# Expert products on four 32-column tiles of TensorE, from weights as loaded

## What is computed

```python
def moe_swiglu(x, w_router, w_gate, w_up, w_down):
    logits = (x @ w_router).astype(jnp.float32)
    top_vals, top_idx = lax.top_k(logits, TOP_K)
    weights = jax.nn.softmax(top_vals, axis=-1)
    combine = jnp.sum(jax.nn.one_hot(top_idx, N_EXPERTS) * weights[..., None], axis=-2)
    out = jnp.zeros_like(x)
    for e in range(N_EXPERTS):
        out = out + combine[..., e:e + 1] * swiglu(x, w_gate[e], w_up[e], w_down[e])
    return out
```

## Time and profile before

| | us |
|---|---|
| median of three runs | 1660.54 (1660.43 to 1660.86) |
| the profiled execution | 1658.83 |
| its span, first to last instruction | 1657.0 |
| TensorE busy in the span | 1598.1 |
| VectorE busy | 1284.6 |
| ScalarE busy | 1027.1 |
| moved by DMA | 464.09 MB |

### The profile page before, as it was taken

One profiled execution on the slowest core, in us unless ns is written; L12 is line 12 of the kernel. 1 busy time (PEld: TensorE's weight loads), 2 busy tenths in 40 slices (PEclk: granted clock), 3 DMA queues, 4 the chain that ended last, 5 costly groups with the idle time before them and its releaser, 6 DMA issues.

```text
span 1657.0 us, 20954 instructions
## 1 busy us (share of the span) xinstructions
PE 1598.1 (96%) x7543; PEld 1327.3 (80%) x7543; DVE 1284.6 (78%) x1060; ACT 1027.1 (62%) x837; POOL 41.3 (2%) x47
## 2 busy tenths in 40 slices
PE   7999999998999979999999999999999999999986
PEld 6887788887788868888888888888888888888865
DVE  5776555557745579889889889889889889889887
ACT  4433543444445457777777777777777777777762
POOL 3011000001000010000000000000000000000011
PEclk9999999999999979999999999999999999999998
DMA  9864555463453219999999999999999999989970
GB/s 368 294 263 132 183 198 182 166 214 127 161 201 102 77 51 361 368 336 356 371 337 361 376 327 352 381 330 351 379 334 352 379 333 366 379 316 368 365 280 26
DMA packets 194867, 464.09 MB, mean 280 GB/s; under 512 B 7456, under 2 KB 7472, under 8 KB 194320
## 3 DMA queue, kind: packets, MB, share of 16 engines
q1 hardware_dynamic: 192448, 453.01, 75.1%
q0 software_dynamic: 2384, 10.60, 1.6%
HBM read 462.53 MB, written 1.05 MB: 280 GB/s over the span
## 4 chain that ended last, share of the span: by engine, by line
PE 87%; DVE 7%; issue 3%; ACT 2%; DMA 1%; ACTq 0%; DVEq 0%
PE ps L1372 83%; DVE wl L858 2%; PE ps L1820 1%; PE ps L1389 1%; DVE acc L896 1%; DVE acc L1301 1%; ACT wh L538 1%; DVE htl L868 0%; DMA ws_raw<-in_gm_w_s_dram 0%; DVE stats L905 0%; PE ps L1700 0%; DVE ysl L1291 0%; ACT L538 0%; PE ps L1721 0%; PE ps L1592 0%
## 5 line engine op out<-in xcount | busy, mean ns | idle before, releaser
L858 DVE TENSOR_TENSOR wl<-raw,wh 128x2048 fp32r<-128x2048 f32 x372 | 844.8, 2288 | 132.1 <-ACT wh L538 131.7
L538 ACT CAST wh<-raw 128x2048 fp32r<-128x2048 f32 x372 | 712.6, 1917 | 263.2 <-PE ps L1372 263.1
L1372 PE MATMUL ps<-wh,xeh 128*128 128x512 f32 x896 | 355.0, 396 | 1.9 <-DVE wl L858 1.9
L1372 PE MATMUL ps<-wh,xel 128*128 128x512 f32 x896 | 350.0, 391 | 0.0
L1372 PE MATMUL ps<-wl,xeh 128*128 128x512 f32 x896 | 349.5, 390 | 0.0
L1372 PE MATMUL ps<-wh,hth 128*128 128x512 f32 x608 | 243.2, 400 | 8.7 <-DVE htl L868 4.4
L1372 PE MATMUL ps<-wl,hth 128*128 128x512 f32 x608 | 239.9, 395 | 0.0
L1372 PE MATMUL ps<-wh,htl 128*128 128x512 f32 x608 | 239.5, 394 | 0.0
L1372 PE MATMUL ps<-wh,bth 128*128 128x512 f32 x560 | 218.7, 391 | 1.8 <-DVE btl L868 1.6
L1372 PE MATMUL ps<-wh,btl 128*128 128x512 f32 x560 | 218.0, 389 | 0.0
L1372 PE MATMUL ps<-wl,bth 128*128 128x512 f32 x560 | 217.9, 389 | 0.0
(11 more groups left out here) (233 smaller groups left out, 1100.1 us busy)
## 6 DMA issues: line engine op xcount, KB each, us to landing
raw<-in_moe_w_gate_dram SPq DMA_DIRECT2D x114, 1024.0 KB, 6.9
raw<-in_moe_w_up_dram SPq DMA_DIRECT2D x112, 1024.0 KB, 7.0
raw<-in_moe_w_down_dram SPq DMA_DIRECT2D x112, 1024.0 KB, 6.3
raw<-in_gm_w_in_dram SPq DMA_DIRECT2D x14, 1024.0 KB, 14.6
raw<-in_ffn_w_gate_dram SPq DMA_DIRECT2D x14, 1024.0 KB, 5.0
raw<-in_ffn_w_up_dram SPq DMA_DIRECT2D x14, 1024.0 KB, 5.9
raw<-in_ffn_w_down_dram SPq DMA_DIRECT2D x14, 1024.0 KB, 4.8
raw<-in_fox_w_in_dram SPq DMA_DIRECT2D x12, 1024.0 KB, 5.1
```

What stands on the lines that cost most here:

```text
L538: nc.scalar.copy(wh[:, gs % SPL], raw[:, gs % RAW]).then_inc(s0["hi"], 1)
L858: nc.vector.tensor_tensor(wl[:, gs % SPL], raw[:, gs % RAW], wh[:, gs % SPL].bitcast(F32), ALU.subtract).then_inc(s0["lo"], 1)
L1372: return nc.tensor.matmul(o, a, b, start=start, stop=stop)
```

## The change

An expert now works on 96 slots (`CAP`), three groups of 32. The weights are not split: TensorE multiplies fp32 by fp32. One matmul has 32 slots as the stationary operand and 256 columns of weights as the moving one, and its output lies in one of four 32-partition strips of a PSUM bank, which places it on one of four 32-column tiles of TensorE. In gate and up (`gate_up`) the 256 columns are 128 of gate and 128 of up. Twelve matmuls cover 96 slots by 1024 columns for one row chunk of 128: strips 0 to 2 hold the three slot groups, strip 3 takes a fourth quarter of the columns for one group after the other; `t`, the strip, is the innermost loop. A block has 96 such matmuls for gate and up and 48 for down.

The 6 slots of `raw` and the room of `wh` and `wl` and two more slots become one ring of 14 slots of 1 MiB for the experts' loop, each with a semaphore of its own; SyncE reloads a slot once its granule has been used 14 granules before. The first 12 loads can go as soon as the slots are free, the last two after the gather.

The tokens of all experts are gathered once, before the loop: VectorE makes `every` (0/1, 256 tokens by 8 experts by 96 slots), TensorE does 64 matmuls of 384 columns, ScalarE and VectorE copy the 16 outputs out in turns to `xt`, and `expert_x` copies the next expert's part to `xe`. The outputs of an expert are unfolded from the four strips (`unfold`: five copies on ScalarE, three subtractions on VectorE) and their weighting moves behind the scatter (`add_weighted`). Hidden values: two SiLU and two multiplications per block, three transposes, one copy to `m_bt`; no `btl`. The loop over blocks is unrolled in the program. The branch for more tokens is taken if an expert has over 96.

Behind the loop ScalarE rounds the three first embedding granules before it unfolds the last expert's output, not after.

The core of the diff; what is left out are buffers, names, and the branch for more tokens:

```diff
+RING = 14
+CAP = 96
+G3 = 32
+    RING_SLOT = (4, 5, 0, 1, 2, 3, 8, 9, 10, 11, 6, 7, 12, 13)
+    GX_BANK = (0, 1, 4, 5, 6, 7, 0, 1, 4, 5, 6, 7, 4, 5, 6, 7)
...
+    def gu_at(j):
+        return G_BLK * j - 2 if j else 0
+    def down_at(j):
+        return G_BLK * j + 8 if j < NJ - 1 else G_EXP - 2
...
+        for idx in range(G_EXP):
+            if idx < RAW:
+                sp.wait_ge(streams[0]["lo"], G_MOE - RAW + 1 + idx)
+            elif idx < RING - 2:
+                sp.wait_ge(streams[0]["used"], G_MOE - (1 if idx < RING - 4 else 0))
+            elif idx < RING:
+                sp.wait_ge(gx_full, 2 * KD)
+            else:
+                sp.wait_ge(streams[0]["used"], G_MOE + idx - RING + 1)
+            ring_load(idx, ring_source(idx, 0))
+        def ring_loads(first, last, base):
+            with sp.Fori(first, last) as e:
                 g0 = sp.snap(G_MOE + e * G_EXP)
-                ex = sp.snap(e - rnd * NE)
-                swiglu_loads(G_MOE, g0, of(moe_w_gate, ex), of(moe_w_up, ex), of(moe_w_down, ex), True)
-                expert_head(g0 + G_EXP, sp.snap((ex + 1) % NE))
-        expert_head(G_MOE, 0)
-        experts(0)
+                ex = sp.snap(e - base)
+                for idx in range(G_EXP):
+                    source = ring_source(idx, ex)
+                    sp.wait_ge(streams[0]["used"], g0 + (idx - RING + 1))
+                    ring_load(idx, source)
...
+        def gathered(done):
             for half in range(2):
-                nc.scalar.mul(ysh[:, half * W:(half + 1) * W], ps[2 + half][:, :], wslot[:, 0:1])\
-                    .then_inc(done, 1)
-        def gathered(n):
-            for q in range(2):
-                act.wait_ge(gx_full, n * 2 - (1 - q))
-                nc.scalar.copy(xeh[:, 4 * q:4 * q + 4, :],
-                               ps[4 + q][:, :].rearrange("p (c t) -> p c t", t=P)).then_inc(gx_hi, 1)
-        def experts(rnd_no):
-            if rnd_no:
-                gathered(1 + rnd_no * (NE + 1))
-            with act.Fori(rnd_no * NE, (rnd_no + 1) * NE) as e:
+                for k in range(0, KD, 2):
+                    n = half * KD + k
+                    act.wait_ge(gx_full, done * (2 * KD) + (n + 1))
+                    nc.scalar.copy(xt[:, k, half * NQ:(half + 1) * NQ], ps[GX_BANK[n]][:, 0:NQ]).then_inc(gx_act, 1)
+        def unfold(ready, hi, fold, done):
+            act.wait_ge(s0["used"], ready)
+            nc.scalar.copy(ysh[0:CAP, 0:W], ps[2][0:CAP, :]).then_inc(hi, 1)
+            nc.scalar.copy(ysh[0:CAP, W:W + 2 * P], ps[3][0:CAP, 0:2 * P])
+            for q in range(3):
+                nc.scalar.copy(y_fold[q * G3:(q + 1) * G3, :], ps[2 + q // 2][CAP:P, q % 2 * 2 * P:(q % 2 + 1) * 2 * P])\
+                    .then_inc(fold, 1)
+            act.wait_ge(fold, done)
+            nc.scalar.copy(ysh[0:CAP, W + 2 * P:D], y_fold[0:CAP, :]).then_inc(hi, 1)
...
+                unfold(g0, y_hi, y_folded, e1 * 3)
+                for j in range(NJ):
+                    n = act.snap(e * NJ + (j + 1))
+                    act.wait_ge(s0["used"], g0 + (gu_at(j) + 4))
+                    nc.scalar.activation(m_sg[:, 0:2 * P].rearrange("p (q n) -> p q n", n=P),
+                                         ps[0][:, :].rearrange("p (q x) -> p q x", x=2 * P)[:, :, 0:P],
+                                         ACT.Silu).then_inc(e_silu, 1)
+                    nc.scalar.activation(m_sg[:, 2 * P:NQ], ps[1][:, 0:P], ACT.Silu).then_inc(e_silu, 1)
+                    act.wait_ge(h_turned, n)
+                    nc.scalar.copy(m_bt[:, j % 2, :, :], ps[4][:, 0:NQ].rearrange("p (c t) -> p c t", t=P))\
+                        .then_inc(bt_ready, 1)
+                    if j == 1:
+                        act.wait_ge(st_full, e1)
+                        nc.scalar.copy(sel_t[0:CAP, :], ps[6][0:CAP, 0:S]).then_inc(st_copied, 1)
...
+        for n in range(SPL):
+            round_hi(n, 1)
+        unfold(USED_TAIL + G_EXP, last_hi, last_folded, 3)
...
+        def gather(done, at_e):
             for half in range(2):
-                for c in range(4):
-                    last = mm(ps[2 + half][:, c * P:(c + 1) * P], zeros[:, :], zeros[:, :], c == 0, c == 3)
-            return last
-            pe.wait_ge(sel_ready, n * (T + 1) - 1)
-            for q in range(2):
-                for c in range(4):
-                    k = slice((4 * q + c) * P, (4 * q + c + 1) * P)
-                    o = ps[4 + q][:, c * P:(c + 1) * P]
+                pe.wait_ge(every_ready, at_e + half)
+                for k in range(KD):
+                    n = half * KD + k
+                    before = [b for b in range(n) if GX_BANK[b] == GX_BANK[n]]
+                    if before:
+                        b = before[-1]
+                        pe.wait_ge((gx_act, gx_dve)[b % 2], done * KD + (b // 2 + 1))
+                    o = ps[GX_BANK[n]][:, 0:NQ]
                     for m in range(T):
-                        mm(o, xh[:, m, k], sel[:, m, :], m == 0, False)
-                        last = mm(o, xl[:, m, k], sel[:, m, :], False, m == T - 1)
-                last.then_inc(gx_full, 1)
+                        one = every[:, m, 4 * half:4 * half + 4, :].rearrange("p e s -> p (e s)")
+                        mm(o, xh[:, m, k * P:(k + 1) * P], one, m == 0, False)
+                        last = mm(o, xl[:, m, k * P:(k + 1) * P], one, False, m == T - 1)
+                    last.then_inc(gx_full, 1)
...
+                def gate_up(j):
                     for half in range(2):
+                        idx = gu_at(j) + 2 * half
+                        slot = landed(idx)
+                        assert landed(idx + 1) == slot + 1
                         for c in range(4):
                             k = 4 * half + c
+                            for q in range(3):
+                                for t in range(4):
+                                    grp, n0 = (t, q) if t < 3 else (q, 3)
+                                    o = ps[q // 2][t * G3:(t + 1) * G3, q % 2 * 2 * P:(q % 2 + 1) * 2 * P]
+                                    last = mm(o.rearrange("p (x n) -> p x n", x=2), xe[:, k, grp * G3:(grp + 1) * G3],
+                                              ring[:, slot:slot + 2, c, n0 * P:(n0 + 1) * P], k == 0 and q != 1,
+                                              k == KD - 1 and q != 0)
+                        last.then_inc(s0["used"], 2)
+                def hidden_turn(j):
+                    pe.wait_ge(e_hid, pe.snap(e * NJ + (j + 1)))
+                    for c in range(3):
+                        last = nc.tensor.transpose(ps[4][:, c * P:(c + 1) * P], m_hb[:, c * P:(c + 1) * P],
                                                    ident[:, :])
+                    last.then_inc(h_turned, 1)
...
+                def down(j, k):
+                    if k == 0:
+                        pe.wait_ge(bt_ready, pe.snap(e * NJ + (j + 1)))
+                    slot = landed(down_at(j) + k)
+                    for kk in range(2):
+                        c = 2 * k + kk
+                        for q in range(3):
+                            for t in range(4):
+                                grp, n0 = (t, q) if t < 3 else (q, 3)
+                                tok = (m_bt[:, j % 2, c, grp * G3:(grp + 1) * G3] if c < 3
+                                       else m_bt[:, j % 2, grp, CAP:P])
+                                last = mm(ps[2 + q // 2][t * G3:(t + 1) * G3, q % 2 * 2 * P:(q % 2 + 1) * 2 * P], tok,
+                                          ring[:, slot, 2 * kk + n0 // 2, n0 % 2 * 2 * P:(n0 % 2 + 1) * 2 * P],
+                                          j == 0 and c == 0 and q != 1, j == NJ - 1 and c == 3 and q != 0)
+                    last.then_inc(s0["used"], 1)
+                def scatter():
+                    for q in range(2 * T):
+                        if q % 2 == 0:
+                            pe.wait_ge(y_lo, pe.snap(e * 2 + (q // 2 + 1)))
+                        scatter_part(SC_BANK[q], q % 2, q // 2).then_inc(sc_full, 1)
+                pe.wait_ge(xe_ready, xe_before(r, e1))
+                gate_up(0)
+                pe.wait_ge(gx_act, gx_before(r))
+                pe.wait_ge(gx_dve, gx_before(r))
+                pe.wait_ge(st_copied, e1)
+                scatter()
+                hidden_turn(0)
                 for j in range(1, NJ):
+                    gate_up(j)
+                    if j == 1:
+                        pe.wait_ge(sc_added, e1 * (2 * T))
+                    down(j - 1, 0)
+                    hidden_turn(j)
+                    if j == 1:
+                        select_turn()
+                    down(j - 1, 1)
+                for k in range(2):
+                    down(NJ - 1, k)
```

More of the change, by code:

```diff
@@ L529, in round_hi @@
                 act.wait_ge(raw_landed2[g], 16)
+            if which and g < SPL:
+                act.wait_ge(s0["used"], USED_TAIL + G_EXP - RING + RING_SLOT.index(RAW + 2 * ss) + 2)
```

(41 more changed lines are left out.)

407 lines of the change are left out of this document (159 added, 248 removed).

## The result

The changed kernel takes 1664.7 us in the median (1662.1 to 1667.3), against 1660.5 for the one before: a ratio of 1.0029, with the interval [1.0019, 1.0039]. So it is slower, by little but measurably. The profiled execution has a span of 1662.7 us.

What follows compares the result with a forecast made beforehand. The prediction took the experts' loop to be bound by TensorE's columns. Span 1657.0 - 70 (loop) + 7 (start) - 5 (end) = 1589 us, plus 1.8 around it and 1.7 to the median: 1592.5 us, range 1565 to 1705.

Steps and rivals of the forecast that it cites:

- rival 2: Issue in a block: each pair of weight load and matmul needs 60 ns, block 18.0 us, program 1696 us; chance 0.15.
- The products: Blocks of the experts' loop: four strips fully beside each other, 144 products in 15.5 us, whole block 16.2 us.
- the charge for the change of form: Each block's transposing turn: 0.33 us for going from strips to the full array and back (bounds 0 and 0.7).
- Rival 1: Products on strips: strict program order lets only neighbouring halves overlap, block 31.7 us, program 2463 us; chance 0.20.
- Rival 3: Weight loads in the experts' loop: a long stretch gives only 356 GB/s, program 1627 us; chance 0.08.
- Start: Before the loop: the single gather for all experts ends near 621 us, costing +7 us.
- end: Behind the loop: earlier embedding rounding saves 6.1 us, longer unfolding costs 1.3 us, net -5 us.
- split: Experts' loop: dropping the weights' roundings and subtractions is worth 2 us at most, as TensorE waited 1.9 us for them.
- The step that failed is the sum: Whole program: 1657.0 - 70 (loop) + 7 (start) - 5 (end) = 1589 us of span, 1592.5 us as median time.
- some gaps at expert borders: Experts' loop: these gaps, with double charge for the change of form, would give 1625 us.

Runs made afterwards that it cites:

- The unread products: Changed kernel with 16 added fp32 products of 256 columns, results never read, at the end of each expert: 1685.9 us, ratio 1.0160.
- light ones: Changed kernel with experts 1 to 7 loading only 128 of the 2048 columns of each weight granule: 1635.4 us, ratio 0.9858.

## Why the prediction was wrong

Forecast were 1592.5 us and, with a chance of 0.64, a faster kernel. It is 4.2 us slower, which had 0.33. The range of 1565 to 1705 held it by luck: its upper part was there for slow issue (rival 2), which did not occur, and not for what happened.

**The products** were right. Block 16.2 forecast, 16.16 measured: 15.68 for 288 matmuls, where 15.5 and half of the charge for the change of form had been set, and 0.48 for three transposes with the change before them. An expert, forecast 115.4, is 115.2 us in the kernel without the branch.

**Rival 1, program order,** is refuted for this kernel by the fours, 6 to 7 ns apart. Its mechanism isn't empty, though. With the same products in another order the block took 23.1 us, so the argument that `t` is innermost was needed. The rule of the Trainium skill that I cited (TensorE: Matmul & The Clock Gate, Part 3, matmuls keep program order in start and end) doesn't forbid what is seen here, four starts in order within 20 ns.

**Rival 2, issue:** a pair each 54.4 ns (15.68 us / 288) for blocks on end; 60 ns is no floor.

**Rival 3, loads,** is refuted by 385 GB/s over 860 us in the kernel without the branch, at a DMA share of 1.02. This lies over the 358 GB/s of the Trainium skill (DMA: Bandwidth & Descriptors, Specifications), now for a long stretch; the measurement decides. I had also read the figure too broadly: the same page of the Trainium skill says, under Bandwidth, that each core gets about 358 GB/s when both cores of an HBM domain stream, and this program runs on one core. In the changed kernel the dips of the rate are the borders.

**Start, end and split** were right within 2 us, the start partly by luck. First product at 619.5 for 621: the gather began at 606.4, 1.6 us later than I had set it, but the granted clock was 0.71 from 608 to 612 and 1.00 from there, where I had set the rise at 615. The end was 4.4 us shorter, for 5. TensorE's 1.9 us of waits for the split are gone.

**The step that failed is the sum.** It adds up what the expert's instructions take and has no term for the branch at its end. It lacks 7 x 10.8 = 75.6 us. 1589 + 75.6 - 2 from the other terms gives 1663, the span measured. Of the 10.8 us some 8.0 are the two stops (5.4 + 2.7 from start to start, less a step) and the remaining 2.8 the half clock behind them. The chances had "some gaps at expert borders" up to 1625 and no mechanism for them. The working had what it takes, in its own words: a block of 288 matmuls with 288 loads of weights, seven in an expert, inside a loop with a branch. It priced the issue of those 4100 instructions (rival 2) and never asked where they come from. In the trace of the kernel before, the fetches are 24 packets in the whole span and none from 730 to 1600 us: its loop ran from the instruction memory. That line of the page, beside a body that grows from 1150 to 4100, was the sign.

The Trainium skill speaks of this, and I hadn't weighed it: Runtime: NRT & Kernel Launch, Instruction fetch mechanics, says that TensorE's instruction memory holds 2048 instructions, filled in blocks of 256 while the program runs straight on, and that a taken branch to code outside the current window of two blocks makes the engine wait for a DMA. The runs here agree with the 2048 and the blocks: 1150 loop without a fetch, 2300 don't, 4100 in a straight line cost nothing, and a packet brought 255 matmuls and loads. They do not agree with a window of two blocks, since the branch back over 1150 instructions, more than four blocks, needed no fetch; the measurement decides. That page has no price for the wait; here the first wait was 2.7 us with free DMA engines and 5.4 behind weights, a second one of 2.7 followed, and then came the clock.

## What to carry to other kernels

Count the instructions of a loop's body on each engine before unrolling it or cutting its products into smaller ones. If it outgrows the instruction memory, write the whole loop out: straight code is fetched ahead of need, and here that alone turned a kernel 0.3% slower than the one before into one 4.4% faster. The bound lies between 1150 and 2300 instructions for TensorE by these runs; for other engines no run shows it. If a branch must stay, put useful long instructions straight ahead of it, and look that no deep queue of loads is full at that moment. The unread products of the experiments cost more than they hid (1685.9 us against 1664.7).

Four strips of unsplit fp32 really work beside each other if consecutive products go to different strips; the same products in another order cost half as much again.

## What was not expected of the hardware

- A branch back to code that has left TensorE's instruction memory stopped the engine for 5.3 to 5.6 us at a DMA rate of 400 GB/s and 2.7 to 3.3 us at 37 GB/s; 17 matmuls later it stopped again, for 2.1 to 3.6 and 1.1 to 2.4 us.
- From within or at the end of the first stop the granted clock was 0.50 for 6.8 us at the first border and 10.2 us at the six others, which cost 2.8 us per border. In the kernel before with longer bodies, stops of 1.4 to 2.1 us left it at 1.00.
- In the changed kernel, TensorE went on 1.7 to 1.9 us after the end of the 16 KiB packet that lay in the first stop, with full loads and with light ones.
- What hides a stop is the time of the last 17 or so matmuls ahead of the branch (an estimate from 2.8 us and 0.161 us each): 13.8 us of work placed 96 matmuls earlier hid none of it.
- Pairs of a weight load and a matmul, with 32 stationary columns, ran at one in 54.4 ns within the blocks.
- Loads of one core moved 385 GB/s over 860 us, and 401 to 409 in windows of 4 us.
- The change from strips to the full array and back cost little: three transposes and the change before them took 0.48 us, where the transposes alone are 0.33.
